# Gate and up projections of a feed-forward stage as seven half-size products in place of eight

## What is computed

```python
h = rmsnorm(x, g_pre_ffn)
f = (jax.nn.silu(h @ w_ffn_gate) * (h @ w_ffn_up)) @ w_ffn_down
return x + rmsnorm(f, g_post_ffn)
```

## Time and profile before

| | |
|---|---|
| median of 3 runs | 3060.55 us |
| profiled execution, first to last instruction | 3065.1 us |
| TensorE (PE) busy | 3009.8 us, 98% |
| VectorE (DVE) busy | 1544.2 us, 50% |
| ScalarE (ACT) busy | 1075.2 us, 35% |
| GpSimd (POOL) busy | 565.5 us, 18% |
| mean granted TensorE clock | 0.996 of full speed |

### The profile page before, as it was taken

One profiled execution on the slowest core, in us unless ns is written; L12 is line 12 of the kernel. 1 busy time (PEld: TensorE's weight loads), 2 busy tenths in 40 slices (PEclk: granted clock), 3 DMA queues, 4 the chain that ended last, 5 costly groups with the idle time before them and its releaser, 6 DMA issues.

```text
span 3065.1 us, 42689 instructions
## 1 busy us (share of the span) xinstructions
PE 3009.8 (98%) x16799; PEld 2580.6 (84%) x16799; DVE 1544.2 (50%) x2780; ACT 1075.2 (35%) x1978; POOL 565.5 (18%) x579
## 2 busy tenths in 40 slices
PE   8989899999999999999999999999999999999998
PEld 7778788888788888888888888888899998899976
DVE  8997654454797730003498652002379765200023
ACT  5766442234355530003155532002235543300012
POOL 4950010000581000000085000000048300100001
PEclk9999999999999999999999999999999999999999
DMA  8866779898654455556655455556565534455553
GB/s 301 277 225 198 254 253 290 291 305 297 219 193 153 137 206 195 194 194 214 220 193 181 136 197 181 194 195 212 189 207 172 166 125 170 152 178 168 178 165 118
DMA packets 173303, 620.09 MB, mean 202 GB/s; under 512 B 20544, under 2 KB 23360, under 8 KB 172592
## 3 DMA queue, kind: packets, MB, share of 16 engines
q1 hardware_dynamic: 172144, 616.96, 59.4%
q10 hardware_dynamic: 960, 0.40, 0.0%
HBM read 478.05 MB, written 139.33 MB: 201 GB/s over the span
## 4 chain that ended last, share of the span: by engine, by line
PE 80%; DVE 3%; DMA 1%; ACT 1%; issue 1%; POOL 0%; SPq 0%; ACTq 0%; POOLq 0%; DVEq 0%
PE PS L942 54%; PE PS L1002 7%; PE PS L1004 7%; PE PS L1003 7%; PE PS L1148 1%; PE PS L976 1%; PE PS L1119 1%; DVE PS L1756 1%; PE PS L1104 1%; DMA out_y_prompt<-x 1%; PE PS L919 1%; DVE y L2116 0%; PE PS L1000 0%; PE PS L1001 0%; DMA u<-in_state 0%
## 5 line engine op out<-in xcount | busy, mean ns | idle before, releaser
L942 PE MATMUL PS<-h_hi,w_hi 128*128 128x512 f32 (+1 forms) x3320 | 1056.8, 351 | 13.6 <-DVE u L2051 6.0
L942 PE MATMUL PS<-h_lo,w_hi 128*128 128x512 f32 (+1 forms) x3320 | 1048.8, 349 | 0.0
L942 PE MATMUL PS<-h_hi,w_lo 128*128 128x512 f32 (+1 forms) x3320 | 1048.8, 349 | 0.0
L942 PEld LDWEIGHTS PS<-h_hi,w_hi 128*128 128x128 f32 x3320 | 587.4, 188 | 96.9 <-issue 18.2
L942 PEld LDWEIGHTS PS<-h_hi,w_lo 128*128 128x128 f32 x3320 | 587.3, 188 | 77.6
L942 PEld LDWEIGHTS PS<-h_lo,w_hi 128*128 128x128 f32 x3320 | 587.6, 188 | 77.1 <-issue 1.4
L840 POOL TENSOR_TENSOR y<-y,prod 128x512 f32<-128x512 f32 (+1 forms) x333 | 431.8, 1325 | 155.9 <-ACT prod L1437 143.0
L1756 DVE SCALAR_TENSOR_TENSOR PS<-u,dw,PS 128x512 f32<-128x512 f32 (+1 forms) x604 | 434.0, 764 | 7.0
L2202 DVE TENSOR_TENSOR f<-PS,tmp 128x512 f32<-128x512 f32 (+1 forms) x88 | 61.6, 700 | 743.4 <-PE PS L942 720.9
L1580 ACT ACTIVATE tmp<-PS 128x512 f32<-128x512 f32 (+1 forms) x88 | 53.3, 605 | 702.1 <-PE PS L942 680.3
L1002 PE MATMUL PS<-w_hi,f_hi 128*128 128x512 f32 x704 | 275.4, 391 | 0.7 <-ACT ostash_d L1394 0.7
(11 more groups left out here) (250 smaller groups left out, 3584.1 us busy)
## 6 DMA issues: line engine op xcount, KB each, us to landing
w_lo<-lo_dram SPq DMA_DIRECT2D x372, 512.0 KB, 4.5
w_hi<-hi_dram SPq DMA_DIRECT2D x372, 512.0 KB, 3.6
w_raw<-in_w_stream SPq DMA_DIRECT2D x124, 512.0 KB, 5.3
hi_dram<-w_hi SPq DMA_DIRECT2D x124, 512.0 KB, 6.0
lo_dram<-w_lo SPq DMA_DIRECT2D x124, 512.0 KB, 5.8
x<-in_x_prompt SPq DMA_DIRECT2D x4, 2048.0 KB, 11.7
xs<-in_x_prompt SPq DMA_DIRECT2D x12, 512.0 KB, 5.3
out_y_prompt<-x SPq DMA_DIRECT2D x3, 2048.0 KB, 11.1
```

Source lines behind the costliest of these rows:

```text
L942: last = nc.tensor.matmul(PS[:, k0 + off, col:col + n], w, x[:, k, c0:c0 + n], start=first and k == 0, stop=stop and k == KT - 1)
```

## The change

The gate and up projections of a feature tile j become one product of a 2 x 2 by a 2 x 2 block matrix. The weights have four quarters: gate and up (first index of `RAWS`) by channels 0 to 511 and 512 to 1023 (second index): A11, A12, A21, A22, each `128x512`. The activations have four: channels 0 to 511 (a) and 512 to 1023 (b) by tokens 0 to 255 (first) and the rest (second, 256 tokens, in block 3 288). Seven products of half the channels and half the tokens replace eight:

| i | weights | activations |
|---|---|---|
| 1 | A11 | a first |
| 2 | A12 | b first |
| 5 | A21 + A22 | a second - a first |
| 6 | A21 + A22 - A11 | b second - (a second - a first) |
| 3 | A12 - (A21 + A22 - A11) | b second |
| 7 | A11 - A21 | b second - a second |
| 4 | A22 | (a first - b first) + (b second - a second) |

Gate of the first tokens is 1 + 2, of the second 1 + 5 + 6 + 3; up of the second 1 + 6 + 7 + 5, of the first 1 + 6 + 7 - 4. Each is again three matmuls per channel tile. GpSimd makes the four sums of weights of every tile in every block, from raw quarters that SP loads (256 KB each, two tiles deep); ScalarE and VectorE split all seven into high and low parts in every block; nothing of gate and up is written back to DRAM. The gain is applied to the transposed activations in place of the weights (`second_out`, into `h32`), and VectorE, ScalarE and GpSimd make and split the activation operands once per block. The outputs are put together by VectorE (`product_out`). The first four products made are 1 and 2 of tiles 0 and 1, whose weights are split during the output projection (`PRE`); the ring of split quarters has WR = 8 places, the split of weights runs AHEAD = 6 products ahead, and product m goes to PSUM bank m % 8 (`bank_of`). VectorE's list for the stage is at the end of the diff.

```diff
@@ sizes, order of the products
-         + ["out"] * KT + ["ffn_gate", "ffn_up"] * FT + ["down"] * FT)
+         + ["out"] * KT + ["down"] * FT)
+KH = KT // 2
+N1 = T // 2
+HW = KH * P
+ORDER = [(0, 1), (0, 2), (1, 1), (1, 2)]
+ORDER += [(j, i) for j in (0, 1) for i in (5, 6, 3, 7, 4)]
+ORDER += [(j, i) for j in range(2, FT) for i in (1, 2, 5, 6, 3, 7, 4)]
+NM = len(ORDER)
+PLACE = {ji: m for m, ji in enumerate(ORDER)}
+A11, A12, A21, A22 = RAWS = (0, 0), (0, 1), (1, 0), (1, 1)
+ALONE = {1: A11, 2: A12, 4: A22}
+USERS = {A11: (1, 6, 7), A12: (2, 3), A21: (5, 7), A22: (5, 4)}
+SUMS = [m for m, (_, i) in enumerate(ORDER) if i not in ALONE]
+PRE = 4
+WR = 8
+AHEAD = 6
+OPS = (1, 2, 5, 6, 3, 7, 4)
+WIDE = (3, 5, 6, 7)
@@ places and banks
+        def bank_of(j, i):
+            return PLACE[j, i] % 8
+        def ring_place(m):
+            return (m - PRE) % WR // 2, slice(m % 2 * HW, m % 2 * HW + HW)
@@ GpSimd
+            def summed_weights(b, m):
+                j, i = ORDER[m]
+                if i == 5:
+                    raw_landed(pool, b, j, A21)
+                    raw_landed(pool, b, j, A22)
+                    one, other, op = raw_of(j, A21), raw_of(j, A22), ALU.add
+                elif i == 6:
+                    pool.wait_ge(ws_ok, len(SUMS) * b + SUMS.index(m))
+                    raw_landed(pool, b, j, A11)
+                    one, other, op = product_sum(m - 1), raw_of(j, A11), ALU.subtract
+                elif i == 3:
+                    pool.wait_ge(ws_ok, len(SUMS) * b + SUMS.index(m))
+                    raw_landed(pool, b, j, A12)
+                    one, other, op = raw_of(j, A12), product_sum(m - 1), ALU.subtract
+                else:
+                    one, other, op = raw_of(j, A11), raw_of(j, A21), ALU.subtract
+                low_place_free(pool, b, m)
+                nc.gpsimd.tensor_tensor(product_sum(m), one, other, op).then_inc(ws_ok, 1)
+            def operand_7(b):
+                pool.wait_ge(hlo_ok, norm_tile(b, last_piece(b), 1) + 1)
+                pool.wait_ge(w_used, G(b, S_F - 1) + 1)
+                t = slice(N1, cols(b))
+                nc.gpsimd.tensor_tensor(op_sum[ext(b)][7][:], h32[:, KH:KT, t], h32[:, 0:KH, t],
+                                        ALU.subtract).then_inc(opsum_pool, 1)
@@ TensorE (removed: first_ffn_steps and feature_major for the gate and up steps)
+            def product(b, m):
+                j, i = ORDER[m]
+                bank, n, o = bank_of(j, i), width(b, i), ext(b)
+                pe.wait_ge(wl_ok, NM * b + m + 1)
+                if j == 0:
+                    pe.wait_ge(op_ok, len(OPS) * b + OPS.index(i) + 1)
+                if m >= 8:
+                    bank_read(pe, b, m - 8)
+                hi, lo = product_hi(m), product_lo(m)
+                x_hi, x_lo = op_hi[o][i], op_lo[o][i]
+                for k in range(KH):
+                    part_k = slice(k * P, k * P + P)
+                    for w, x, first, stop in ((hi, x_hi, True, False), (hi, x_lo, False, False),
+                                              (lo, x_hi, False, True)):
+                        last = nc.tensor.matmul(PS[:, bank, 0:n], w[:, part_k], x[:, k, :],
+                                                start=first and k == 0, stop=stop and k == KH - 1)
+                last.then_inc(m_used, 1)
@@ ScalarE
+            def high_weights(b, m):
+                if m >= NM:
+                    return
+                j, i = ORDER[m]
+                high_place_free(act, b, m)
+                if i not in ALONE:
+                    act.wait_ge(ws_ok, len(SUMS) * b + SUMS.index(m) + 1)
+                    src = product_sum(m)
+                else:
+                    raw_landed(act, b, j, ALONE[i])
+                    src = raw_of(j, ALONE[i])
+                A(product_hi(m), src, ACT.Copy).then_inc(wh_ok, 1)
+            def product_out_by_act(b, m):
+                j, i = ORDER[m]
+                if i == 1:
+                    one_out(b, j)
+                if i == 2:
+                    out_made(act, b, j, "gate1")
+                    A(f[:, j, 0:N1], f[:, j, 0:N1], ACT.Silu).then_inc(silu_ok, 1)
+                if i == 3:
+                    out_made(act, b, j, "gate2")
+                    two = f[:, j, N1:cols(b)]
+                    A(two, two, ACT.Silu).then_inc(silu_ok, 1)
-                    if kind == "ffn_gate":
-                        if r - S_F >= 4:
-                            act.wait_ge(z_dve, by_dve(b, r - 3))
-                        A(tmp[:, (r - S_F) // 2 % 2, 0:c], z(b, r)[:, 0:c], ACT.Silu).then_inc(z_act, 1)
@@ VectorE
+            def second_out(b, tt):
+                dve.wait_ge(tr_done, norm_tile(b, tt, 1) + 1)
+                r = rows(tt)
+                TT(h32[:, :, toks(tt)], turned(b, tt)[:, :, r],
+                   gn[:, 1, :].unsqueeze(2).broadcast_to([P, KT, r.stop]), ALU.mult).then_inc(hlo_ok, 1)
+            def operand_sums(b, c):
+                late_piece = c.stop > P
+                dve.wait_ge(hlo_ok, norm_tile(b, last_piece(b) if late_piece else 2, 1) + 1)
+                dve.wait_ge(w_used, G(b, S_F - 1) + 1)
+                t5, t6 = op_sum[ext(b)][5], op_sum[ext(b)][6]
+                main, t = slice(c.start, min(c.stop, N1)), slice(N1 + c.start, N1 + c.stop)
+                if c.stop > N1:
+                    nc.vector.tensor_copy(t5[:, :, N1:c.stop], h32[:, 0:KH, T:TX])
+                TT(t5[:, :, main], h32[:, 0:KH, N1 + main.start:N1 + main.stop], h32[:, 0:KH, main],
+                   ALU.subtract).then_inc(opsum_ok, 1)
+                dve.wait_ge(opsum_ok, 4 * b + 2 * late_piece + 1)
+                TT(t6[:, :, c], h32[:, KH:KT, t], t5[:, :, c], ALU.subtract).then_inc(opsum_ok, 1)
+            def low_weights(b, m):
+                if m >= NM:
+                    return
+                j, i = ORDER[m]
+                dve.wait_ge(wh_ok, NM * b + m + 1)
+                low_place_free(dve, b, m)
+                if i in (5, 6):
+                    dve.wait_ge(ws_ok, len(SUMS) * b + SUMS.index(m) + 2)
+                src = raw_of(j, ALONE[i]) if i in ALONE else product_sum(m)
+                TT(product_lo(m), src, product_hi(m).bitcast(F32), ALU.subtract).then_inc(wl_ok, 1)
+            def product_out(b, m):
+                j, i = ORDER[m]
+                n = width(b, 3)
+                f1, f2, main = f[:, j, 0:N1], f[:, j, N1:N1 + n], f[:, j, N1:T]
+                both, up2 = part[:, 0, 0:n], part[:, 1, 0:n]
+                ps = {r: PS[:, bank_of(j, r), 0:width(b, r)] for r in range(1, 8)}
+                if i in OUTS:
+                    dve.wait_ge(m_used, NM * b + m + 1)
+                if i == 2:
+                    dve.wait_ge(one_ok, FT * b + j + 1)
+                    TT(f1, ps[2], main, ALU.add).then_inc(outs, 1)
+                if i == 6:
+                    dve.wait_ge(one_ok, FT * b + j + 1)
+                    if j:
+                        out_made(dve, b, j - 1, "f1")
+                    if ext(b):
+                        nc.vector.tensor_copy(part[:, 0, N1:n], ps[6][:, N1:n])
+                    TT(both[:, 0:N1], ps[6][:, 0:N1], main, ALU.add).then_inc(outs, 1)
+                    out_made(dve, b, j, "both")
+                    TT(f2, ps[5], both, ALU.add).then_inc(outs, 1)
+                if i == 3:
+                    out_made(dve, b, j, "part2")
+                    TT(f2, ps[3], f2, ALU.add).then_inc(outs, 1)
+                if i == 7:
+                    TT(both, ps[7], both, ALU.add).then_inc(outs, 1)
+                    out_made(dve, b, j, "up")
+                    TT(up2, ps[5], both, ALU.add).then_inc(outs, 1)
+                if i == 4:
+                    out_made(dve, b, j, "up2")
+                    TT(both[:, 0:N1], both[:, 0:N1], ps[4], ALU.subtract).then_inc(outs, 1)
+                    silu_made(dve, b, j, "gate2")
+                    TT(f2, f2, up2, ALU.mult).then_inc(outs, 1)
+                    silu_made(dve, b, j, "gate1")
+                    out_made(dve, b, j, "up1")
+                    TT(f1, f1, both[:, 0:N1], ALU.mult).then_inc(outs, 1)
-            def gain_raw(g):
...
-                    TT(w, w, gn[:, 1, :].unsqueeze(2).broadcast_to([P, KT, P]), ALU.mult).then_inc(w_gain_ok, 1)
...
-                    if kind == "ffn_up":
-                        j = (r - S_F) // 2
-                        dve.wait_ge(z_act, by_act(b, r))
-                        TT(f[:, j, 0:c], z(b, r)[:, 0:c], tmp[:, j % 2, 0:c], ALU.mult).then_inc(z_dve, 1)
+                        whole, last = slice(0, width(b, 3)), slice(P, width(b, 3))
+                        residual(b, 0, 0)
+                        residual(b, 1, 0)
+                        residual(b, 2, 0)
+                        low_weights(b, PRE)
+                        second_out(b, 0)
+                        if ext(b):
+                            residual(b, 3, 0)
+                        second_out(b, 1)
```

(47 more changed lines are left out.)

518 lines of the change are left out of this document (356 added, 162 removed).

## The result

The changed kernel takes **3221.0 us** (median of 4 runs, 3220.3 to 3226.4) against 3061.1 us of the kernel before on the same chip: ratio **1.0527**, 95% interval 1.0512 to 1.0542. The prediction was 3215 us, 3065 to 3310.

What follows compares the result with a forecast made beforehand. TensorE bounded the kernel before, and VectorE would bound the changed one. 72 + 2 (VectorE's tiles) + 72 (entry) + 4 (clock) + 6 (exit) = +156 us; 3065.1 + 156 - 4.5 = 3217, say 3215 us, range 3065 to 3310.

Steps and rivals of the forecast that it cites:

- the forecast's own case: Gate/up stages: VectorE becomes the bound and entries grow, +156 us in all, about 3215 us; chance 0.58.
- TensorE's part: Gate/up matmul stream: 84 matmuls at 0.120 us, 10.08 us per tile in blocks 0 to 2; 87 us less in all.
- VectorE's tile: VectorE per feature tile: 9.6 us of work and pauses plus 2.4 of collisions, 12.0 us; 12.3 in block 3.
- The pauses for ScalarE: Behind products 2 and 3, VectorE waits for ScalarE's Silu and high part: 2.1 us per tile.
- The collision as the deciding term: VectorE instructions with two SBUF inputs meet GpSimd's four sums per tile: 2.4 us, bounds 0 and 4.4.
- Start-to-start spacing: VectorE instructions priced by spacing of starts, 7.3 us per tile; full durations would give 8.6.
- Entry: Start of each gate/up stage: longer operand chain leaves TensorE idle, +18 us per block, +72 in all, ends 14 and 24.
- The clock: TensorE at stage entry: one fall to 1.2 GHz after the idle gap, +1 us per block, +4 in all.
- Exit: End of each stage: weights for the first down step land late, +3 us in block 0, +1 in each other, +6.
- the rival in which each tile's pause lowers it: Pauses of some 2 us per tile lower TensorE's clock: over 500 us more; chance 0.10 together with another slower case.
- VectorE over 90% busy: Sign that the forecast is right: VectorE busy over 90% of the gate/up stage.
- The rival "VectorE keeps up": Gate/up stages: collisions cost under 0.5 us per tile, TensorE stays the bound, about 3056 us; chance 0.15.

Runs made afterwards that it cites:

- e2: The changed kernel with GpSimd's sums of weights behind the first twelve products replaced by writing a constant: 3075.9 us, ratio 1.0049 to the kernel before.
- e4: e1 with VectorE, in place of GpSimd, making the sums of weights behind the twelfth product: 3094.8 us, ratio 1.0104 to the kernel before.
- e1: The changed kernel with ScalarE making the high parts of weights 7 products ahead in place of 6: 3161.2 us, ratio 1.0328 to the kernel before.
- e7: e4 with VectorE, in place of GpSimd, making operand sums 7 and 4 and the sums of weights 9 to 11: 3082.5 us, ratio 1.0074.
- e9: e7 without the sums of weights from product 9 on, GpSimd writing a constant in their place: 3060.1 us, ratio 0.9992 to the kernel before.

## Why the prediction was right

The time, 3221 against 3215, came from the forecast's own case, and its terms can be checked one by one. In spans the sum gives 3065.1 + 156 = 3221.1 and 3219.5 was measured; the forecast's median is lower since 4.5 us were taken off for a slow profiled execution before, and the one after stands 1.5 us below its median.

- **TensorE's part**, 0.120 us per matmul, 10.08 per tile: held. In e2 TensorE has no gap behind the entry.
- **VectorE's tile**, 12.0 us predicted: 11.83 measured, in block 3 12.36 (starts 2863.74 and 2876.10 of two tiles) against 12.3. The pauses for ScalarE were right (2.1), the collisions a little less than thought (2.1, not 2.4). Blocks 0 to 2 then lose 22 x 0.93 = 20.5 us each in place of 24.
- **The collision as the deciding term**: held by e2 (-145 us without it) and e4. That the terms add did not hold: e1 took most of the 2.1 us of pauses from a tile and got 0.6 back (a tile of 11.24 between TensorE's waits at 1300.71 and 1311.95, for 11.83), since the collisions grew from 2.1 to 3.3 per tile (47 us in 14.2 tiles).
- **Start-to-start spacing** in place of full durations for VectorE: held. The section of the Trainium skill that the prediction cites for full durations ("VectorE: DVE Perf Modes", "The DRAIN you can't avoid") goes on to say that a next instruction that is not held starts earlier, so it does not stand against these rows. By full durations e4's list would be 11 x 0.69 + 9 x 0.42 = 11.4 us per tile, and TensorE, with 10.1 to 10.2 per tile, would have waited; it was busy 159.78 of 160 us.
- **Entry**, +18 us per block with ends 14 and 24: 4.82 + 2.12 + 12.72 = 19.7 us of gaps in block 1, 22.2 in block 0, 19.8 in block 2. Product 0 came at +4.8 (predicted 4.7), product 1 at +11.0 (11), product 4 at +30.7 where 24.9 to 29.4 was given. The 5.8 us above 24.9 are made up, to 0.3 us, of four things. GpSimd's part is 4.1 us (e7: 12.72 to 8.60), within the 4.5 allowed for it. VectorE took gate1 from the bank of product 3 at 1197.29, +17.1 and not +15.5: 17 matmuls of products 1 and 2 still ran at 1.2 GHz, 17 x 0.093 = 1.6 us, a price of the clock that the sum had beside the path. The pause of 1.00 us for ScalarE's high part behind gate1 (row 1198.71) was priced in the steady state and not here. Against these, the prediction counted all three last low parts (1.9 us) in front of product 4, and in the code it waits only for the first: in e7 it starts at 1170.25, with the pair from 1169.41 half done. That is 1.2 too much. Block 3 was the worst, with 5.51, 1.79 and 15.58.
- **The clock**: it fell at each entry, twice, not once. In block 1 the 12 matmuls behind the 4.82 us gap stand 0.21 us apart (1.2 GHz), 17 of products 1 and 2 too (granted clock 0.50 from 1193 to 1195), and again the first 23 behind the 12.72 us gap; 52 matmuls at 0.093 more are 4.8 us, where 1 was taken. The four entries have 50, 52, 51 and 33 such matmuls, some 17 us together, part of it beside VectorE's work. The pauses of 1.5 us once per tile left it at 1.00 (window 1240 to 1400), so the rival in which each tile's pause lowers it is out.
- **Exit**: 2.4 us in block 0 (L2428), predicted 3; loads of quarters in 3.7 us, never late.
- Per block 46, 44, 44 and 22 us were predicted and 40.8, 42.7, 41.8 and 29.2 measured: the steady state was taken 3.5 us too high in blocks 0 to 2, and the entry too low, above all in block 3. The errors cancel to 156 against 154.4.
- One sign to look for was wrong: VectorE over 90% busy. It is busy 131.26 of 160 us, 82%. An engine whose tile is made up of work and of pauses in a ping-pong sets the pace without looking full.

The rival "VectorE keeps up" said 3056 us. e2, where it does keep up, stands at 3076, because its entry was priced at 72 us. From e2: 3061 - 87 + X = 3076 gives X = 102 us for entry, clock and exit of four blocks. Gaps on op_lo and op_lox in e2 are 60.7 + 21.1 = 82 us, the slow clock some 16 (counted in the same way), the exit a few. With 18 us less of gaps (e9: 48.4 + 15.6 = 64) the total is the kernel before again. That these terms fill the 102 us speaks for the saving of 87 us, and so does TensorE's stream in e2, without a gap from 500 to 650 (150.00 of 150 us busy), at 0.120 us per matmul. One part of the loss ate it (the entry), and the other (VectorE against GpSimd, 145 us) made the result.

What stays open: whether the last rows can be taken sooner by another order of VectorE's list, and whether the entry can be hidden behind other TensorE work, for instance a first tile in eight products, which does not need the operand sums. Neither was tried.
